# A fused transformer kernel's opening: weight halves made as they land, the input's low halves ahead of its square sums, the first scores inside the second half of the values

## The reference, cut to what matters

```python
hn = rms_norm(h, attn_norm[i])                       # h = x
q, k, v = jnp.split(hn @ w_qkv, 3, axis=-1)
q = apply_rope(q.reshape(B, S, 2 * H, d), cos, sin)  # cos, sin of the positions' angles
k = apply_rope(k.reshape(B, S, 2 * H, d), cos, sin)
s = jnp.einsum('bqhd,bkhd->bhqk', qb, k) * scale
a = softmax(q1 k1) - lam_full * softmax(q2 k2)
o = jnp.einsum('bhqk,bkhe->bqhe', a, v)
```

## Time and profile before

| | |
|---|---|
| median of 3 runs | 2097.93 us (2096.63 to 2098.93) |
| profiled execution, its own time | 2095.74 us |
| its span, first to last instruction | 2094.0 us |
| PE busy | 2043.6 us (98%) |
| DVE busy | 1226.8 us (59%) |
| ACT busy | 942.3 us (45%) |
| POOL busy | 905.9 us (43%) |
| mean granted TensorE clock | 0.992 |

### The profile page before, as it was taken

The page is one execution under the profiler, slowest core; times in us unless marked ns, Lnnn a source line. Parts: engine busy times, 40 slices in busy tenths (PEclk is TensorE's granted clock), DMA queues, the critical chain, the costliest instruction groups (busy, mean ns, idle before and its releaser), DMA issues.

```text
span 2094.0 us, 28726 instructions
## 1 busy us (share of the span) xinstructions
PE 2043.6 (98%) x9976; PEld 1683.2 (80%) x9976; DVE 1226.8 (59%) x1842; ACT 942.3 (45%) x1494; POOL 905.9 (43%) x660
## 2 busy tenths in 40 slices
PE   6999999999999989899999999999999999999999
PEld 5777788888887878788888887878888788888887
DVE  7487867646275679856636267538879473213222
ACT  5456545434245467644524245434742544323222
POOL 4322135554446431144545446444215454455454
PEclk9999899999999999999999999999999999999999
DMA  4322122322223210022332323222003222232323
GB/s 148 101 76 76 41 81 91 109 93 96 97 98 112 90 61 32 31 81 91 100 102 91 100 92 119 91 81 88 34 31 101 85 97 90 90 104 97 101 90 111
DMA packets 52612, 183.21 MB, mean 87 GB/s; under 512 B 6432, under 2 KB 6688, under 8 KB 52512
## 3 DMA queue, kind: packets, MB, share of 16 engines
q1 hardware_dynamic: 51072, 177.76, 25.8%
q10 hardware_dynamic: 1440, 4.07, 0.5%
HBM read 176.04 MB, written 2.10 MB: 85 GB/s over the span
## 4 chain that ended last, share of the span: by engine, by line
PE 58%; issue 23%; POOL 14%; DVE 4%; ACT 1%; POOLq 0%; DVEq 0%; ACTq 0%
PE PS L530 56%; POOL wlo L522 14%; PE PS L759 1%; DVE acc L1597 0%; DVE AR L1760 0%; DVE ptlo L1768 0%; DVE AR L2234 0%; DVE nmax L1716 0%; DVE Blo L2238 0%; ACT Bhi L1100 0%; DVE Blo L1590 0%; DVE X L1633 0%; DVE AR L2232 0%; ACT AR L1171 0%; DVE qklo L1706 0%
## 5 line engine op out<-in xcount | busy, mean ns | idle before, releaser
L522 POOL TENSOR_TENSOR wlo<-raw,whi 128x512 fp32r<-128x512 f32 x656 | 905.7, 1404 | 1174.9 <-ACT whi L1074 1173.8
L530 PE MATMUL PS<-Bhi,whi 128*128 128x512 f32 x2368 | 935.0, 395 | 24.7 <-POOL wlo L522 15.4
L530 PE MATMUL PS<-Blo,whi 128*128 128x512 f32 x2368 | 924.1, 390 | 0.0
L530 PE MATMUL PS<-Bhi,wlo 128*128 128x512 f32 x2368 | 923.9, 390 | 0.0
L1074 ACT ACTIVATE whi<-raw 128x1024 fp32r<-128x1024 f32 x328 | 345.4, 1056 | 515.4 <-PE PS L530 445.9
L530 PEld LDWEIGHTS PS<-Bhi,whi 128*128 128x128 f32 x2368 | 445.5, 188 | 134.5 <-issue 30.2
L530 PEld LDWEIGHTS PS<-Bhi,wlo 128*128 128x128 f32 x2368 | 445.8, 188 | 94.2
L530 PEld LDWEIGHTS PS<-Blo,whi 128*128 128x128 f32 x2368 | 446.0, 188 | 89.8 <-issue 0.5
L1581 DVE TENSOR_TENSOR AR<-PS,R 128x512 f32<-128x512 f32 x170 | 115.3, 689 | 236.2 <-PE PS L530 224.7
L1633 DVE TENSOR_TENSOR X<-X,PS 128x512 f32<-128x512 f32 x88 | 60.3, 687 | 227.0 <-PE PS L530 226.3
L1878 DVE SCALAR_TENSOR_TENSOR AR<-AR,par_sb 128x511 f32<-128x511 f32 x88 | 117.6, 1336 | 8.8 <-ACT AR L1307 8.8
(11 more groups left out here) (230 smaller groups left out, 2030.2 us busy)
## 6 DMA issues: line engine op xcount, KB each, us to landing
raw<-in_weights SPq DMA_DIRECT2D x328, 512.0 KB, 3.2
AR<-AR SPq DMA_DIRECT2D x56, 64.0 KB, 2.0
X<-in_xT ACTq DMA_DIRECT2D x4, 512.0 KB, 7.7
out<-X SPq DMA_DIRECT2D x8, 256.0 KB, 3.1
AR<-in_pT ACTq DMA_DIRECT2D x2, 512.0 KB, 3.9
par_sb<-in_parameters ACTq DMA_DIRECT2D x1, 322.0 KB, 4.5
AR<-in_positions ACTq DMA_DIRECT2D x1, 256.0 KB, 9.0
con_sb<-in_constants ACTq DMA_DIRECT2D x1, 198.5 KB, 8.9
```

The lines of the kernel that those rows point to most:

```text
L522: ins = pool.tensor_tensor(wlo[:, j, c], raw[:, j % RAWS, c], f32(whi[:, j, c]), ALU.subtract)
L530: return pe.matmul(out, w, x, start=start, stop=stop)
```

## The change

It rewrites the order of the opening on four engines and changes no product.

```diff
@@ the order of the value tiles, by half
+        VALUES = {("v1", 0): (2, 3, 0, 1), ("v1", 1): range(TB), ("v2", 0): range(TB), ("v3", 0): range(TB)}
@@ PE
             first_pair("qk1a", "attn0")
+            values("v1", "attn0", 4, T, (0, 1))
             pe.wait_ge(consts_ready, 3)
-            values("v1", "attn0", 4, T, (0,))
             norm_sum("attn0")
-            values("v1", "attn0", 4, T, (1,), halfway=lambda: spread_norm("attn0"))
-            values("v1", "attn0", 4, T, (2, 3))
+            values("v1", "attn0", 4, T, (2,), halfway=lambda: spread_norm("attn0"))
+            values("v1", "attn0", 4, T, (3,))
+            values("v1", "attn0", 4, T, (0, 1), half=1)
             scores(1, 0)
-            values("v1", "attn0", 4, T, range(4), half=1)
+            values("v1", "attn0", 4, T, (2, 3), half=1)
@@ ACT
-            act.dma_start(par_sb[:, :], par).then_inc(par_in, 16)
+            act.dma_start(par_sb[:, 0:16], par[:, 0:16]).then_inc(par_in, 16)
...
+            act.dma_start(par_sb[:, 16:NPAR], par[:, 16:NPAR]).then_inc(rest_in, 16)
+            act.wait_ge(consts_ready, 1)
+            act.activation(nmax[:, 4:5], eps[:, 0:1], ACT.Copy)
+            for s in range(2):
+                high(s, s, 0)
             act.wait_ge(par_in, 16)
             for m in range(KC):
                 if m % 2 == 0:
                     act.wait_ge(x_in[m // 2], 16)
-                    high(m // 2, m // 2, m // 2 // RAWS)
-                square_and_high("attn0", m, m % 2)
-
+                act.activation(chunks(Bhi[0])[:, m, :], X[:, m, :], ACT.Copy,
+                               scale=gain("attn_norm", 0, m)).then_inc(xhi_ready, 1)
+            for s in range(2, 4):
+                for m in range(4 * s - 8, 4 * s - 4):
+                    act.activation(first_square(m), X[:, m, :], ACT.Square).then_inc(sq_ready, 1)
+                high(s, s, 1)
+
+            act.wait_ge(sq_used, 2)
             for t in range(2):
                 used("qk1a", 0, t)
                 swap_halves("qk1a", t, t)
+            act.wait_ge(rest_in, 16)
             root("attn0")
@@
             values("v1", (0,), 4, T)
+            for t in range(2):
+                q_high(t, 0, t)
             exps(1, 0)
             values("v1", (1,), 4, T)
@@ DVE
             for q in range(4):
                 dve.wait_ge(x_in[q], 16)
                 for m in (2 * q, 2 * q + 1):
-                    low_and_add("attn0", m, m % 2)
+                    low("attn0", m)
+            for m in range(KC):
+                dve.wait_ge(sq_ready, m + 1)
+                tt(acc[:, :], acc[:, :], first_square(m), ALU.add).then_inc(sq_used, 1)
+                dve.wait_ge(sq_used, m + 1)
...
             dve.wait_ge(consts_ready, 3)
+            inverse_root("attn0")
...
             factor("attn0")
+            values_low("v1", (0,), T)
...
             for t in range(2):
                 q_low(t, 0, t)
-            values_low("v1", (0,), T)
             maxima(1, 0)
```

More of the change, by code:

```diff
@@ L267, in build, with first_square @@
         ones = one.broadcast_to((P, P))
+        def first_square(m):
+            return ar(0, KC)[:, (m + 2) % KC, :]
         rC, rS = ar(0)[:, 0, :], ar(512)[:, 0, :]
@@ L323, in build @@
         ple_added, pp_done = sem("ple_added"), sem("pp_done")
+        rest_in = sem("rest_in")
         mixc_ready = sem("mixc_ready")
@@ L1141, in values @@
                         used(stage, 0, hf * slabs + q)
-                        if stage == "v1" and hf == 0 and q == 1:
-                            for t in range(2):
-                                q_high(t, 0, t)
                     if hf == 0:
@@ L1150, in values @@
                             act.wait_ge(pad_ready, {"v2": 4, "v3": 8}[stage])
-                    for t in range(TB):
+                    for t in VALUES[stage, hf]:
                         bank, _ = tile_of(stage, 0, hf * TB + t)
@@ L1606, in clear_sum, with inverse_root @@
                 own.wait()
+            def inverse_root(norm):
+                dve.wait_ge(root_ready, NORMS.index(norm) + 1)
+                dve.reciprocal(rcol[:, :], rootc[:, :]).then_inc(rcol_ready, 1)
             def factor(norm):
                 n = NORMS.index(norm)
-                dve.wait_ge(root_ready, n + 1)
-                dve.reciprocal(rcol[:, :], rootc[:, :]).then_inc(rcol_ready, 1)
+                if norm != "attn0":
+                    inverse_root(norm)
                 dve.wait_ge(rspread, n + 1)
@@ L1641, in values_low @@
                 for hf in halves:
-                    for t in range(TB):
+                    for n, t in enumerate(VALUES[stage, hf]):
                         bank, _ = tile_of(stage, 0, hf * TB + t)
-                        dve.wait_ge(vhi_ready, n0 + hf * TB + t + 1)
+                        dve.wait_ge(vhi_ready, n0 + hf * TB + n + 1)
                         if stage == "v1":
@@ L1936, in _ @@
             dve.wait_ge(par_in, 16)
-            own.step(tt(gfm[:, :], cpar("final_norm", 0, KC), cpar("g_mix", 0, KC), ALU.mult))
-            own.step(ts(nsink[:, :], cpar("sinks", 0, 16), -1.0, None, ALU.mult))
             for q in range(4):
@@ L1941, in _ @@
                 for m in (2 * q, 2 * q + 1):
-                    low_and_add("attn0", m, m % 2)
+                    low("attn0", m)
[3 more added lines that the diff above has]
+                dve.wait_ge(sq_used, m + 1)
+            dve.wait_ge(rest_in, 16)
+            own.step(tt(gfm[:, :], cpar("final_norm", 0, KC), cpar("g_mix", 0, KC), ALU.mult))
+            own.step(ts(nsink[:, :], cpar("sinks", 0, 16), -1.0, None, ALU.mult))
             dve.wait_ge(con_in, 16)
```

## The result

| | before | changed |
|---|---|---|
| median, runs of the comparison | 2095.13 us (20) | 2100.33 us (20) |
| ratio, 95% interval | | 1.0025, 1.0018 to 1.0032 |
| span of the profiled execution | 2094.0 us | 2095.9 us |
| end of the first values (my mark) | 80.73 us | 84.33 us |

The changed kernel is 5.2 us slower (3.8 to 6.7 by the interval); I had forecast 3.8. The 5.2 lies just beyond the 0.2% (4.2 us) that I called indistinguishable, and the interval reaches to both sides of it. One run of each kernel was far slower than the rest (5230.45 and 2403.21 us) and is left out of the ratio. Before has a median of 2095.13 over 20 runs where the three shown gave 2097.93.

What follows compares the result with a forecast made beforehand. PE was taken to wait on slabs and banks held back by DVE's angles through ACT's program order. Values done 4.3 us later (85.0 against 80.73), less 0.5, on a median of 2097.93 gave 2101.7 us; range 2097 to 2106.

Steps and rivals of the forecast that it cites:

- The start: Opening up to the square sums: PE's second start at 13.85 instead of 16.59, sums at 37.15, worth some 5 us.
- The chain: Sums, root, reciprocal, angles, sine, slabs 6 to 9, bank emptying in a queue; bank 2 free at 61.4, PE idle 9.85 us.
- The lower bound for the angles: DVE's chain of angles with POOL idle: 6.7 us taken, from bounds of 6.7 and 10.6.
- The second gap: PE's wait of 7.0 us for an emptied value bank, after one tile of the second half, until 61.4.
- The clock: Behind PE's two waits the clock falls to the low level for 4.5 us, costing 2.1 us.
- the gap stays short of cost: Rival: PE's clock stays up or returns at once behind the gap, 2.1 us less, 2099.6; 15%.
- A wait at the scores: Rival: late rope tables make PE wait 1.5 us at the scores, clock stays low; 2104.7 to 2107.6, 18%.
- The opening wins: Rival: angles don't hold slab 6 because DVE makes them from 30 on; values done near 79.5, 2096.2; 10%.
- The drain at a table switch: Rival at ACT's root: a table switch costs more than its load, 2103.0; 5%. The skill's rule adds 1.38 us per switch.
- an average run before has some 0.5 us less to lose: Last step of the sum: the profiled slow stretch at the start was the shortest, so 0.5 us is subtracted.
- 52%: Chance of a result within 0.2% of the kernel before; slower had 42%, faster 6%.
- the table load behind the sums: ACT's root table load waits for the square sums, putting 1.28 us into the chain from sums to reciprocal.

Runs made afterwards that it cites:

- number 10: Number 9 with ACT's wait for the second parameter transfer also moved ahead of the swap copies; 2088.61 us, 0.9969 of the kernel before.
- number 7: The opening part of the change alone, with the order of the kernel before from the square sums on; 2094.77 us, 1.0001 of the kernel before.
- number 1: The changed kernel with DVE's reciprocal of the root put back behind the chain of angles; 2092.69 us, 0.9991 of the kernel before.
- number 3: The changed kernel with PE's square sums taken behind slab 2 again, reciprocal still ahead of the angles; 2094.34 us, 0.9997 of the kernel before.
- number 2: The changed kernel with ACT emptying the first half's value banks ahead of the high halves of slabs 8 and 9; 2093.98 us, 0.9995 of before.
- number 4: The changed kernel with 36 unused matmuls in PE's two gaps, 12 and 24, to price the clock; 2098.4 us, 1.0019 of the kernel before.
- number 5: The changed kernel with the changes of number 1 and number 2 together; 2090.39 us, 0.9980 of the kernel before.
- number 6: The changed kernel with one parameter transfer instead of two, the waits on the second gone; 2099.3 us, 1.0018 of the kernel before.
- number 8: The changed kernel with ACT's wait for the second parameter transfer moved ahead of the first pair's swap copies; 2098.68 us, 1.0020 of before.
- number 9: Number 5 with the rope tables ahead of the low halves of the values on DVE; 2090.12 us, 0.9976 of the kernel before.

## Why the prediction was right, and what was off

**The start.** ACT free at 6.54 (forecast 6.8), first matmul 10.76 (10.7), second start 13.57 (13.85), low rate until 17.15, 3.6 us (3.4 to 6, 4.5 taken), sums at 36.59 (37.15). The second start is right in kind: slab 1's low half, made at 13.52, released it. The first is luck: GpSimd had made slab 0's low half by 10.16, and PE waited to 10.76 for DVE's first low half of the input, a wait that the forecast doesn't have. The runs of the same opening had the low rate for 3.1 us (13.84 to 16.99, number 10) to 6.1 (13.61 to 19.75, number 7), so the range was about right. Their mean with the changed kernel's is 4.5, as taken; the trace of the changed kernel got a short one.

**The chain.** It holds step by step. Sums to the reciprocal's end 39.45 - 36.59 = 2.86 (2.85 forecast); angles to the sine 6.6 (6.7); sine to slab 6's high half 2.58 (2.57). The lower bound for the angles was the right choice: in number 1, with POOL beside their first step, that step alone took 1.47 against 0.40, and in number 7 the chain took 8.7. Numbers 1 and 3 show the cause by two different routes, and number 2 the second one, ACT's order at the bank. The second gap ended at 60.48 (61.4): 0.6 of the 0.9 is the earlier sums, the rest small terms, such as slabs on POOL of 2.48 (2.54) and slab 9 landed 3.2 after slab 7 was made (3.4).

**The clock.** 4.5 us at 0.50, as in the forecast, and 2.2 us by number 4 (2.1). The one tile between the two gaps ran at the low rate already, 2.9 us instead of the 1.4 that I took; it lay inside the wait for the bank and cost nothing, and made the second wait 5.26 instead of 7.0. The rival "the gap stays short of cost" falls.

**The other rivals.** A wait at the scores didn't appear in the changed kernel (`qklo` done at 69.9, scores at 72.4), and did as soon as PE came earlier, in number 5. "The opening wins" was named with its place, the reciprocal ahead of the angles, and values done near 79.5; number 1 moved it and found 79.18. The drain at a table switch that the Trainium skill gives (ScalarE: Activation LUTs, "What ACT_TABLE_LOAD costs") is not in this trace: the root starts 1.30 after its load of 1.28, as in the earlier trace rows.

**What was off is the size, in the sum's last step.** The mark moved 3.6, less than the 4.3 forecast, while the medians moved 5.2, more than the 3.8 that I made of it. So the step from the mark to the medians, "an average run before has some 0.5 us less to lose", had the wrong sign. Its reasoning overlooked that PE before waits once more behind the start, 0.38, 0.81 and 0.31 us at 25.05, 27.52 and 30.89, all for DVE; a longer slow stretch ahead of these would have been taken up by them. That is argued from the trace, no run shows it. Over the eleven kernels the difference of the medians exceeds that of the marks by 1.0 us on average (-1.1 to 2.0 single):

| | mark, us against before | median ratio, as us of 2095 |
|---|---|---|
| changed | +3.6 | +5.2 |
| 1 / 2 / 3 | -1.6 / -3.1 / -1.5 | -1.9 / -1.0 / -0.6 |
| 4 / 6 / 8 | +2.1 / +2.8 / +2.7 | +4.0 / +3.8 / +4.2 |
| 5 / 7 | -3.1 / -0.5 | -4.2 / +0.2 |
| 9 / 10 | -6.6 / -7.3 | -5.0 / -6.5 |

Each entry of the last column is uncertain by about 2 us, and each mark comes from one execution, in which the low rate at the start alone moves it by up to 1.4 (3.0 us more of it at 0.47). So I can say that the marks order the kernels as the ratios do, bar a few neighbours, and that the opening's shift reaches the end of the run. A cost close behind the mark can be ruled out: the slab that GpSimd starts at 203.66 before starts 3.4 later in the changed kernel, 1.7 earlier in number 1 and 7.3 earlier in number 10, within 0.3 of what the marks say. Part of the gap in the changed kernel is its own profile: its slow start was 0.9 us shorter than the mean, worth 0.4 of the mark, and that execution took 2097.69, 2.6 below the median of its kernel, where before's took 2095.74, 0.6 above. Whether the rest is before's profile or a cost in the low stretches further on stays open; no run was made for it. The step from the mark to the medians decided on which side of the 0.2% the change came out: with the mark's 3.6 the change would have lain inside the 0.2%, where I had put 52%, and not at 0.25%.

**One price was right with a wrong reading of its freedom.** I took the table load behind the sums as a given of the new order. Numbers 6 and 8 show that it comes from the second parameter transfer's wait, written directly ahead of the root: a side effect of splitting a transfer that gained nothing itself. The 1.3 us are shown for the root; that they would have come through to the bank or the mark is not (number 8).

## What to carry to other kernels

An engine that works in program order makes every early wait a queue: before moving a step that waits for another engine ahead of independent work, look at what stands behind it on that engine and who needs it, here 6.6 us of angles behind a reciprocal of 0.18. When a stall is removed, name the next wait before counting the gain; here it went from the angles to the bank to the scores. Numbers 1 and 2 moved the mark by 5.2 and 6.7 us each alone and by 6.7 together, and the next 3.5 us came only with the scores' tables (number 9). And where a change speeds up the start, move the constants and emptying steps of the other engines with it, or the gain is given back at the first place where they meet.

## What the runs showed of the hardware

- A wait written ahead of an activation can end up on its table load. With one wait for the sums ahead of the root, the load (1.28) ran 4 us early and the activation waited; with a second wait (for a transfer issued at 4.66 that took 8.5 us) written directly ahead, the load took the wait for the sums, and 1.34 us entered the chain from the sums to the root. The second load, ahead of the sine, waited for nothing in either (39.19, 6.9 us ahead of its activation).
- VectorE beside a working GpSimd, in number 9 while slabs 8 and 9 were made:

```profile
53.81 0.68 DVE L1704 TENSOR_TENSOR AR<-PS,AR 128x512 f32<-128x512 f32 x1
54.41 1.25 DVE L1705 TENSOR_TENSOR AR<-AR 128x512 f32<-128x512 f32 x1
55.70 1.67 DVE L1708 TENSOR_TENSOR AR<-AR 128x512 f32<-128x512 f32 x1
```

  The product with PSUM kept its 0.68, the two that read SBUF twice took 1.25 and 1.67 where the changed kernel, with GpSimd idle, has 0.68 and 0.69. The Trainium skill (SBUF — State Buffer, "Who interferes with whom") says as much of products with both inputs in SBUF, and the trace agrees.
- The low stretch of the earlier trace rows is found in the other kernels too, elsewhere and of another length. TensorE in the changed kernel:

```profile
230.00:236.00 6.00, 3.56 (x14) 0.70 0.46 131
236.00:242.00 6.00, 4.81 (x12) 0.50 0.01 3
```

  and in number 10:

```profile
224.00:230.00 6.00, 3.69 (x8) 0.50 0.23 82
230.00:236.00 6.00, 6.00 (x32) 0.81 0.00 0
```

  Further ones lie around 870 and 1530 us. Between them the changed kernel's slabs on GpSimd start later than those of before by 3.6 us (right behind the opening), 0.2 (at 788 us), 3.9 (at 1346) and 1.95 (from 1554 to the end). The span of one profile, 2095.9 against 2094.0, is therefore no measure of a few us; a mark ahead of these stretches, and the median of many runs, are.
